# RWKV-7 and gated delta scans in one kernel: the 64x64 systems of direction two are formed transposed, the solver takes two head pairs with both directions at a time, and the RWKV scan follows four steps behind instead of eight

## What is computed

```
def rwkv7_scan(r, w, k, v, kk, b_vec, s0):
    def step(state, inp):
        r_t, w_t, k_t, v_t, kk_t, b_t = inp
        sa = -jnp.einsum('bhvk,bhk->bhv', state, kk_t)
        state = (state * w_t[:, :, None, :] + sa[..., None] * b_t[:, :, None, :]
                 + v_t[..., None] * k_t[:, :, None, :])
        return state, jnp.einsum('bhvk,bhk->bhv', state, r_t)
...
for d in range(2):          # both directions, context first, then the latent tokens
    ...
        o, state = rwkv7_scan(flip_seq(r, d), flip_seq(decay[:, :, d], d), ...)
        outs[i] = outs[i] + flip_seq(o, d)
```

## Time and profile before

| | |
|---|---|
| median of 3 runs | 3989.17 us (3984.3 to 3995.16) |
| span of the profiled execution | 3990.6 us, mean TensorE clock 0.931 of full speed |
| busy, share of the span | PE 87%, PEld 70%, DVE 53%, ACT 17%, POOL 20% |
| stage rprep, POOL's first load to the barrier's end | 2821.8 to 3232.4 us |
| stage scan, its 20 iterations | 3232.4 to 3723 us |

### The profile page before, as it was taken

How to read it: one execution, slowest core, us unless ns; L and a number is a source line. 1 busy time by engine, 2 the same in 40 slices (tenths; PEclk the granted TensorE clock), 3 DMA queues, 4 the chain that set the end, 5 groups by cost and what they waited for, 6 DMA issues and landing times. The chain is left out here.

```text
span 3990.6 us, 64126 instructions
## 1 busy us (share of the span) xinstructions
PE 3488.3 (87%) x28192; PEld 2775.3 (70%) x28192; DVE 2133.2 (53%) x2308; ACT 662.1 (17%) x1079; POOL 791.3 (20%) x817
## 2 busy tenths in 40 slices
PE   6999999999998989799999999999567645677798
PEld 3777777777887878688888888876355535676376
DVE  2477777743334555544453353339688835332564
ACT  2122222212000001211110010012233301221100
POOL 0111111111000000034005125000574789000000
PEclk8999999999999999899999999998689867888799
DMA  9444444444332453322232222328478698777243
GB/s 398 143 155 145 163 149 148 151 166 166 119 119 98 176 188 132 114 91 88 84 111 90 85 103 105 125 108 301 130 197 217 165 231 169 180 227 205 69 175 106
DMA packets 359077, 607.72 MB, mean 152 GB/s; under 512 B 136440, under 2 KB 244080, under 8 KB 330128
## 3 DMA queue, kind: packets, MB, share of 16 engines
q1 hardware_dynamic: 305488, 472.23, 37.6%
q0 software_dynamic: 21712, 92.42, 7.1%
q10 hardware_dynamic: 31600, 38.99, 2.8%
HBM read 469.17 MB, written 134.39 MB: 151 GB/s over the span
## 5 line engine op out<-in xcount | busy, mean ns | idle before, releaser
L182 PE MATMUL front_ps<-b_hT,p_wb 128*128 128x512 f32 x4224 | 979.7, 392 | 6.8 <-PEq L94 6.8
L182 PEld LDWEIGHTS front_ps<-b_hT,p_wb 128*128 128x128 f32 x4224 | 790.0, 188 | 187.5 <-issue 20.6
L1772 PE MATMUL in_ps<-b_hT,in_wb 128*128 128x512 f32 (+1 forms) x3264 | 749.7, 390 | 13.4 <-DVE in_wb L1759 13.4
L1772 PEld LDWEIGHTS in_ps<-b_hT,in_wb 128*128 128x128 f32 (+1 forms) x3264 | 606.7, 187 | 147.5 <-DVE in_wb L1759 13.6
L1757 DVE CAST in_wb<-in_raw 128x2048 fp32r<-128x2048 f32 (+1 forms) x68 | 82.7, 1216 | 535.4 <-PE in_ps L1772 530.5
L170 DVE CAST p_wb<-p_raw 128x2048 fp32r<-128x2048 f32 x88 | 108.0, 1227 | 430.5 <-PE front_ps L182 420.2
L813 POOL DMA_DIRECT2D front_mwb<-in_w_ada x128 | 101.3, 796 | 794.8 <-PE front_mps L823 790.0
L1772 PEld LDWEIGHTS in_ps<-b_hc,in_wb 128*128 128x128 f32 (+1 forms) x1728 | 211.4, 189 | 3.2
L1772 PE MATMUL in_ps<-b_hc,in_wb 128*128 128x256 f32 (+1 forms) x1728 | 212.7, 283 | 0.0
L172 DVE TENSOR_TENSOR p_wb<-p_raw,p_wb 128x2048 fp32r<-128x2048 f32 x88 | 201.8, 2293 | 3.0
L1211 PE MATMUL mid_ps<-mid_wb,b_hT 128*128 128x512 f32 x768 | 178.6, 393 | 13.4 <-DVE mid_wb L1196 13.4
(11 more groups left out here) (456 smaller groups left out, 4347.6 us busy)
## 6 DMA issues: line engine op xcount, KB each, us to landing
p_raw<-in_w_in_tiles SPq DMA_DIRECT2D x88, 1024.0 KB, 6.1
in_raw<-in_w_in_tiles SPq DMA_DIRECT2D x67, 1024.0 KB, 4.8
front_mwb<-in_w_ada POOLq DMA_DIRECT2D x128, 512.0 KB, 5.0
open_wb<-in_w_ada_groups SPq DMA_DIRECT2D x32, 1024.0 KB, 11.3
g_scr<-gprep_ob SPq DMA_DIRECT2D x8, 3474.0 KB, 11.6
merge_raw<-in_w_branch_units SPq DMA_DIRECT2D x32, 512.0 KB, 4.6
mid_raw<-in_w_o_parts SPq DMA_DIRECT2D x32, 512.0 KB, 3.7
last_raw<-in_w_out_parts SPq DMA_DIRECT2D x32, 512.0 KB, 3.7
```

What stands on the lines that cost most here:

```text
L182: last = self.nc.tensor.matmul(self.ps[:, n % 2, :], self.wb[:, n % 2, x, kt, :], self.hT[:, y, kt, :], start=kt == term == 0, stop=kt == ...
L1772: last = self.nc.tensor.matmul(self.ps[0:width, n % 3, first:end], self.wb[:, n % 2, x, kt, 0:width], h[:, y, kt, :], start=kt == term == ...
```

## The change

1. **Storage.** The RWKV systems get a tensor of their own, `r_systems`, of shape (pair, direction, half, chunk, 64, W) with W = 96: rows of 96 numbers, of which the last 64 hold the system and the first 32 a second copy of blocks that the solver writes. `load_inverse` in the scan loads rows of 96.
2. **Transposed.** For direction two the system is formed transposed (`turned_products`: 48 matmuls of 64 columns for each half in place of 24 of 128), so that the solver treats both directions alike.
3. **Batches.** A solver batch of RWKV is two head pairs with both directions (`solve_pairs`, 2 x 2 x 2 x 12 = 96 systems), so there are four of them. Three run in rprep after the two delta batches, each as soon as its own pairs have been stored; the fourth runs in the scan. The load picks the 64 numbers out of each row of 96; there are three copies at the end instead of two; the products' temporary lies in the unused corner of the image.
4. **LAG = 4.** Four iterations of delta alone, eight with both, four of RWKV alone. The last four fold two delta tiles each (`tiles_at`).
5. **Delta outputs** are summed in the working bank of their half after VectorE took the values, and `advance` waits until ScalarE has stored them (`outputs`). The freed bank belongs to RWKV alone.

```
@@ solver @@
+def images_of(r_systems, batch):
+    return r_systems[PAIRS * batch:PAIRS * (batch + 1)].rearrange("q d h c s x -> (q d h c) (s x)")
+def solve_pairs(nc, pool, link, m, r_systems, batch, before):
...
+    pool.dma_start(full[:, :, HC:W], images_of(r_systems, batch).rearrange("p (i j) -> p i j", j=W)[:, :, HC:W]).then_inc(m.n_in, 16)
+    pool.wait_ge(m.n_in, before * 16 + 16)
...
@@ rwkv_prep, gpsimd @@
-                for n, (batch, d) in enumerate(((0, 0), (0, 1), (1, 0), (1, 1))):
-                    if batch == 1 and d == 0:
-                        for u in range(3):
-                            pool.wait_ge(m.stored[u], m.STORED * len(range(u, RP, 3)))
...
-                    begin(nc, pool, link, solver, systems, batch, d, n)
-                    if n < 3:
-                        end(nc, pool, link, solver, systems, batch, d)
+                for batch in range(RP // PAIRS - 1):
+                    for u in range(3):
+                        pool.wait_ge(m.stored[u], m.STORED * len(range(u, 2 * PAIRS * (batch + 1), 3)))
+                    pool.wait_ge(solver.y_out, 16 * (batch + 2))
+                    pool.sem_inc(solver.tick, 1)
+                    solve_pairs(nc, pool, link, solver, r_systems, batch, batch + 2)
@@ scans @@
-LAG = 8
+LAG = 4
+FOLDS = GH // LAG
...
-                end(nc, pool, first.link, first, systems, 1, 1)
...
+                before.finish(pool)
+                solve_pairs(nc, pool, Link(pool, second.chain), second, r_systems, RP // PAIRS - 1, 0)
@@ scans, tensor @@
-                        if STEPS[n][2]:
-                            g.state_outputs(pe, n, 0)
                         g.values(pe, n)
...
+                    if in_g(n) and STEPS[n][2]:
+                        g.outputs(pe, n, 0)
+                        g.outputs(pe, n, 1)
                     if in_g(n):
                         g.advance(pe, n, 0)
@@ DeltaScan.advance @@
-            if g == 1:
-                self.state_outputs(pe, k, g)
-            self.value_outputs(pe, k, g)
+            pe.wait_ge(self.s["o_out"], 4 * (k - NCC) + 2 * g + 2)
```

More of the change, by code:

```diff
@@ L2653, in turn, with rows_of, solve @@
     link(ops.tensor_copy(full[:, near, far], flip(full[:, near, near])))
[L2656 to L2665, removed]
+def rows_of(systems, d):
+    return systems[d]
+def solve(nc, pool, link, m, systems, d, before):
+    pool.dma_start(m.rows, rows_of(systems, d)).then_inc(m.n_in, 16)
     pool.wait_ge(m.n_in, before * 16 + 16)
-    substitute(nc.gpsimd, link, m, d, range(0, SPLIT))
@@ L3436, in middle @@
                 for h in range(2):
-                    own, other, off, diag = quarter(h, d)
-                    last = self.nc.tensor.matmul(self.px[own, q, :], self.inv[other, k % 3, d, q, diag], self.inv[other, k % 3, d, q, off],
-                                                 start=True, stop=True)
+                    own, other = quarter(h, d)[0:2]
+                    first, last_cols = self.inv[other, k % 3, d, q, 0:HC], self.inv[other, k % 3, d, q, C:W]
+                    last = self.nc.tensor.matmul(self.px[own, q, :], last_cols if d else first, first if d else last_cols, start=True, stop=True)
         last.then_inc(self.s["mid_ps"], 1)
@@ L3447, in offdiagonal, with inverse @@
                 for h in range(2):
-                    own, other, off, diag = quarter(h, d)
-                    last = self.nc.tensor.matmul(self.px[own, q, :], self.inv[own, k % 3, d, q, off], self.mid[own, q, :],
-                                                 start=True, stop=True)
+                    own = quarter(h, d)[0]
+                    last = self.nc.tensor.matmul(self.px[own, q, :], self.inv[own, k % 3, d, q, C:W] if d else self.inv[own, k % 3, d, q, 0:HC],
+                                                 self.mid[own, q, :], start=True, stop=True)
         last.then_inc(self.s["off_ps"], 1)
+    def inverse(self, k, d):
+        return self.inv[:, k % 3, d, :, 0:C] if d else self.inv[:, k % 3, d, :, HC:W]
     def term(self, bank, q, h, lhs, rhs, at, first, end):
@@ L3505, in values @@
                 for h in range(2):
-                    last = self.term(self.work[d], q, h, self.inv[:, k % 3, d], self.y[:, d], h, True, True)
+                    last = self.term(self.work[d], q, h, self.inverse(k, d), self.y[:, d], h, True, True)
             last.then_inc(self.s["u_ok"], 1)
@@ L3812, in _ @@
                 before.finish(sp)
-                sp.dma_start(second.rows, rows_of(systems, 2, 0)).then_inc(second.n_in, 16)
                 before.finish_small(sp)
                 r.load(sp, 0)
-                sp.wait_ge(first.y_out, 64)
-                sp.dma_start(first.rows, rows_of(systems, 2, 1)).then_inc(first.again, 16)
                 for n in range(NCH + LAG):
@@ L3829, in _ @@
                         sp.wait_ge(second.y_out, 16)
-                        sp.wait_ge(first.y_out, 80)
+                        sp.wait_ge(first.y_out, 16 * (RP // PAIRS + 1))
                         for m in range(3):
@@ L3954, in _ @@
                     if n == 0:
-                        r.start(dve)
+                        r.start(dve, before)
                         out.start(dve)
```

188 lines of the change are left out of this document (107 added, 81 removed).

## The result

The changed kernel takes 4107.79 us (median of 4 runs, 4100.25 to 4112.65) where the kernel before takes 3990.28 us (4 runs on the same chip): a ratio of 1.0291, 95% interval 1.0272 to 1.0309. The forecast was 4110 us, 4040 to 4190. The profiled execution took 4103.0 us, its span is 4101.3 us (before 3990.6), its mean granted clock 0.921 (before 0.931). So there are 110.7 us to be found.

A forecast was written before the change was run, and what follows sets the result against it. The prediction took RWKV's start, set by POOL's solver, and then twelve iterations paced by the SP queue's load chain as the bound. It summed 3990.6 + 58 (later start) + 62 (longer iterations) = 4110 us, range 4040 to 4190.

The forecast's parts named there:

- The solver's chain: POOL's RWKV batches: no batch's load is hidden now, four cost 20 us each, so RWKV starts 58 us later.
- The load's price: POOL's load of 6144 pieces of 256 B: about 20 us, as 10.6 + 10, scaled from the `front_mwb` load.
- the one gain: Rprep: POOL waits only for pairs 0 and 1, so RWKV's first load is issued at 3031 instead of 3064, 33 us.
- The scan begins 123 us later: Barrier after rprep: POOL's third RWKV batch moves it from 3232 to about 3355, with TensorE idle meanwhile.
- Twelve iterations, 62 us more: Scan from RWKV's start to the end: 364 us against 302, with iterations 7 to 10 at 36 us each.
- the load chain: SP queue in the scan: piece-by-piece waits in `RwkvScan.load` pace iterations with both recurrences; chain 28.1 us before, 34.7 after.
- the sign that I named: Scan iterations n = 7 to 10: near 36 us, with the SP queue never waiting for `free`.
- Delta outputs in working banks: Scan iterations: ScalarE's copies now waited for ahead of `advance`; at most 2 us an iteration either way, hidden, counted as 0.
- turned products: Rprep: 24 more matmuls for each pair, below 2 us of PE, hidden behind POOL, counted as 0.
- The load of pieces: Rival on POOL's batch loads: they are dear, 40 us each, 4 x 20 more, total 4190 us; chance 0.10.
- Joined iterations: Rival on the scan: not load-bound, 30 us in place of 36, with 12 us loads; 4045 down to 4010; chance 0.12.
- the faster case: Rival: the eight iterations with both recurrences take 22.5 us each, with cheap loads and stores; 3965 us; chance 0.05.

The follow-up runs named there:

- e2: Changed kernel with its third RWKV batch solved behind the barrier, in the scan, LAG = 4 kept: 4108.85 us, ratio 1.0283 to the kernel before.
- e3: Changed kernel with the third RWKV batch solved behind the barrier and LAG = 8: 4055.9 us, ratio 1.015 to the kernel before.
- e4: Changed kernel with LAG = 8, third batch solved in the scan, and both scan-solved batches loaded by the SP queue at the scan's begin: 4024.8 us, ratio 1.0069.
- e8: Changed kernel with LAG = 8, two batches solved in the scan, SP-loaded, and POOL's first RWKV batch held until pairs 0 to 3 are stored: 4030.43 us.
- e5: Changed kernel without the waits between the pieces inside RwkvScan.load: 4125.03 us, ratio 1.0335 to the kernel before.
- e6: Kernel before the change, without the waits between the pieces inside RwkvScan.load: 4021.44 us, ratio 1.0073 to the kernel before.
- e1: Changed kernel with LAG = 8 in place of 4, nothing else: 4091.18 us, ratio 1.0239 to the kernel before.
- e9: Changed kernel with delta operand loads of steps 6 to 11 carrying one head of eight, output wrong: 4055.02 us, ratio 1.0154 to the kernel before.
- e7: Changed kernel with LAG = 8, two batches solved in the scan, SP-loaded, and direction two formed straight, not transposed: 4024.67 us, ratio 1.0086.

## Why the prediction was right, point by point

The total is nearer than the working deserves. The two terms of the sum were 58 and 62 us and came out at 35 and 76: the one was 23 us too high, the other 14 too low, and that 4110 stands beside 4107.8 is luck.

**The solver's chain: right, with terms off on both sides.** That no batch's load is hidden any more and that RWKV starts later was shown in the trace, by e2 (an early scan changes nothing) and by e3 to e4 (two loads hidden, 31 us back). RWKV starts 35 us later instead of 58. Against my sum: loads 57.7 us instead of 4 x 20 = 80 (-22.3); stores with a load behind them 44.7 instead of 12 + 12 + 2 = 26 (+18.7), the barrier alone 12.1 where I had 2; computing 298.2 instead of 309 (-10.8); the rest (first load at 3028.1 for 3031, last store to SP 10.5 for 11, SP to RWKV 16.9 for 21.5) -8.0. The load's price was the largest wrong term: its row of comparison, `front_mwb` with 796 ns for 512 pieces, does not scale. POOL's instruction for 6144 pieces takes 2.24 us, 0.36 ns a piece. The fit in the Trainium skill ("DMA: Bandwidth & Descriptors", Anatomy of one DMA) gives an estimate of 5.6 us for one such load. The measured 12.3 to 17.2 us disagree, with the core moving 184 to 244 GB/s meanwhile. They lie between that estimate and my 20 us.

**The first load 33 us earlier is "the one gain": counted fully, worth little.** It came (36 us), but I took VectorE's and POOL's speeds as given. Beside a solving POOL the loop of rprep gets some 17 us longer (medians 3240 and 3223) and POOL's batches too. e8 gives up the early start and loses 10 us at the median, within the noise. In the change this is covered by POOL's longer chain; in e4 the longer loop ends the stage, and the scan begins 16 to 27 us later than in the four profiles with before's stage.

**The scan begins 123 us later: 112 measured, and without a price of its own** (e2), as I had it: what counts is the solver.

**Twelve iterations, 62 us more: 76 measured, size nearly right, cause wrong.** Iterations 4 to 6 took 94.9 us for 86.5, 7 to 10 took 151.3 for 144, n = 11 27.1 for 27, the last four 104.6 for 107. The step that failed is "iterations with both recurrences go by the load chain, because `RwkvScan.load` waits piece by piece". The chain's length I had right (34.7 forecast, 35.4 measured), but its waits are not what makes the iteration long: without them both kernels get slower (e5, e6), and the sign that I named, a queue that never waits for a free buffer, did not come (7.1 us of such waits in n = 8 to 10). The bytes are: in the common stretch 69.8 MB move in place of 56.6. About 11 MB of that are delta operands and inverses of four more steps, 2.3 MB the wider rows of RWKV's inverses (e1 has those alone, 58.9 MB). Of the 73 us between before and after in this stretch, 52 go when 12.7 MB go (e9), some 18 would be joined work and folds, and 3 are what remains at LAG = 8 (e1) for wide inverses, working banks and all else; single profiles scatter by as much as the last two.

**Delta outputs in working banks, turned products: 0.** Right for both: at LAG = 8 the first is within those 3 us and their scatter, and was not tried by itself; e7 shows nothing for the second.

**The rivals.** The load of pieces was cheaper than forecast, not dearer. Joined iterations did not come down to 30 us, those of n = 7 to 10 take 37.8 on average, and 22.5 us, on which the faster case hung, never came near.

## What to carry to other kernels

Before work is moved into a stretch, add up the bytes that the stretch moves and divide by the rate that its rows show: here 14.6 MB more at an unchanged 196 GB/s give 75 us, and 76 were measured. It is a first estimate and no law: the rate was 187 to 214 GB/s in the kernels of this document, and taking 12.7 MB away gave back 52 us and not the 64 that 199 GB/s would make of them. A serial chain on one engine is lengthened by each of its own transfers that no other queue starts early; count the gaps (40.6 to 102.4 us), not only the computing (287 to 298 us). And an idle stretch of GpSimd beside a busy VectorE is not free time: where it was filled, both were slower.

## What the runs showed of the hardware

- VectorE's product of two SBUF tiles of 128x768 takes 0.96 us alone and up to 2.6 us in the part of the stage in which GpSimd solves, mostly 1.1 to 1.9; a product of 128x1536 out of PSUM takes 1.76 us in either case.
- Taking away waits between loads lowered the rate of transfer, from 204 to 187 GB/s in the one kernel and from 199 to 191 in the other. I had not expected a queue that pauses to be the faster one; why is open.
- TensorE stops 34 to 39 times in RWKV's stretch without a wait that the profile shows, and their sum differs from kernel to kernel: 67.3 us before, 90.7 there without the waits between loads, 87.3 in the changed kernel, 53.9 in that with 12.7 MB less. Why is open.
- A load on GpSimd's queue with 64 pieces of 256 B in each of 96 partitions occupies GpSimd for 2.24 us and lands in 13.8 us (median); the same bytes in one piece for each partition land in 10.4, and 1.5 times the bytes in 13.9, all beside other transfers.
